# Sums of squares made inside the output products, one phase for two norms, and a new order in the products' opening turns

## Chip, core and metric

The kernel runs on one core of a Trainium2 chip. The time is device microseconds of one launch. A profiled execution gives a second number, its span, from the first to the last instruction of the program. Engines: PE is TensorE, DVE is VectorE, ACT is ScalarE, POOL is GpSimd, SP is SyncE, which issues most loads.

## The reference

Two blocks in a row on 512 tokens of width 1024, all in float32. The first puts 16 meta tokens ahead (528 tokens), runs a pooling mixer and an HGRN2 mixer, each on the RMS norm of the residual stream `h`, and norms the result. The second computes six modulation vectors from `c`, then attention and a product-key expert layer (PEER), each on a modulated norm.

```python
for i in range(DEPTH):                       # first block
    hn = rmsnorm(h, norm_w[i])
    h = h + (pool_mixer if i == 0 else hgrn2_mixer)(hn, ...)   # each ends in (...) @ w_out
x = rmsnorm(h[:, N_META:], final_norm_w)
mod = silu(c) @ w_ada + b_ada                # second block
h1 = rmsnorm(x, norm1_g) * (1.0 + scale1) + shift1
x = x + gate1 * (attention(h1) @ w_o)
h2 = rmsnorm(x, norm2_g) * (1.0 + scale2) + shift2
x = x + gate2 * peer(h2, ...)
```

with `rmsnorm(x, w) = x * rsqrt(mean(x * x) + EPS) * w`, the mean over the 1024 features of a token.

## The kernel before

Activations lie transposed: features on the 128 partitions, `KC` = 8 chunks of them, tokens along the free side. `hT` is `h` (8 x 528), `xT` is `x` (8 x 512). The program is a row of phases. Each has one instruction block per engine and ends in a barrier of all engines, so the next phase begins when the last engine is through. In order: load, scalars, norm0, pool, **pool_out**, **norm1**, hgrn, **hgrn_out**, gains, **final** norm, **mod1**, latent, two phases of attention heads, **attn_out**, **mod2**, peer (1369 of the 3219 us). The bold ones are touched.

`norm_phase` (L249) is one norm. ScalarE squares the even chunks (L274), VectorE squares the odd ones and adds each pair (L300, L302), TensorE multiplies a matrix of ones with the four pair sums (L292), which leaves the sum over features on every partition. Then ScalarE takes the root (L276), VectorE the reciprocal (L304) and scales the 8 chunks (L306). In mod1 and mod2 ScalarE adds a shift to each chunk (L281). In norm1 it makes the high part of each (L285; a float32 is split into two rounded parts), and the low parts are subtractions, chunks 0 to 3 on GpSimd (L318) and 4 to 7 on VectorE (L311).

`product_phase` (L328) multiplies a weight matrix with the mixer's output and adds the product to the residual, in 8 turns m of 128 output features. `kc` is 16 in pool_out and hgrn_out, 8 in attn_out. Per turn: SP loads w(m) (L364) and, where modulation is computed ("ada"), two pieces of `w_ada` (L369), the second only when VectorE has used up the previous turn's; ScalarE makes the high part wh(m) (L408); GpSimd subtracts for the low part wl(m) (L423); TensorE makes three products for each k, wh x rh, wh x rl, wl x rh (L394), once wl(m) is there; VectorE makes ada(m) in 8 chained operations (L453, L455), then adds the product to the residual, in two halves of 264 tokens (L1983, attn_out: L2052 with a gate), and an ada result of 3 columns to `mod` (L442). Two w buffers: w(m+2) is issued when wl(m) is done, but it stands in SP's queue behind both ada pieces of turn m+1. The high parts rh of the right side come from ScalarE before turn 1 (L411), the low parts rl from VectorE, all 16 or 8 of them, before its ada(0) (L434); in turn 0 TensorE waits for rl k by k.

## Time and profile before

| | us |
|---|---|
| median of 3 runs (range) | 3217.63 (3217.52 to 3218.79) |
| the profiled execution: time, span | 3220.95, 3219.2 |
| pool_out, from its first load to the next phase | 285.5 to 409.5 |
| norm1, up to hgrn's first instruction | 409.5 to 433.5 |
| hgrn_out with gains | 1150.5 to 1275.3 |
| final and mod1, up to latent's first matmul | 1275.3 to 1310.7 |
| attn_out | 1775.1 to 1831.2 |
| mod2, up to peer's first matmul | 1831.2 to 1849.6 |
| peer | 1849.6 to 3219 |
| busy: TensorE, VectorE, GpSimd, ScalarE | 79%, 66%, 36%, 31% of the span |

A timeline row gives start and length in us, engine, line, operation, tile written <- tiles read, shape, count; in square brackets the idle time ahead of it and what ended that. Rows of one kind in a row are merged, so a length can cover several instructions with what they waited for. A length holds the time from an instruction's start to its end, also when it stands still between.

### The profile page before, as it was taken

To read this page: it belongs to the slowest core of one execution; us is meant where nothing else is said; L and a number is where in the kernel's file an instruction comes from. 1 tells how busy PE (TensorE), PEld (TensorE's weight loads), DVE (VectorE), ACT (ScalarE), POOL (GpSimd) and SP (SyncE) were. 2 spreads that over 40 slices of the span, in tenths; PEclk is the share of its full clock that TensorE was granted. 3 is DMA by queue.
4 is the path that set the end of the run, shared out by engine and by line. 5 is a ranking of instruction groups with operands and counts; after the bars stand their busy time and mean duration, and the time that the engine had idled before them with its cause. 6 is when DMAs were issued, how large, how long until landed. Compare 5 with 4: busy or idle time off the path is not lost. (4 is left out here: it accounts for less than half of the span.)

```text
span 3219.2 us, 36203 instructions
## 1 busy us (share of the span) xinstructions
PE 2555.9 (79%) x12276; PEld 1759.3 (55%) x12276; DVE 2108.6 (66%) x3964; ACT 997.9 (31%) x2010; POOL 1170.2 (36%) x952
## 2 busy tenths in 40 slices
PE   6998969999999968767799688966766677766676
PEld 5998959889988858324466533322322232222222
DVE  6356646666666675466534327788887788878876
ACT  2222145555555521232223212222222222222221
POOL 2443345555455522011100214444444444444442
PEclk8999988889898979878899899998888888888888
DMA  3233621111111034100110249999999999999998
GB/s 99 87 95 99 190 59 50 43 52 46 52 52 46 27 122 140 39 28 0 40 40 1 79 171 400 415 427 427 410 427 426 423 403 427 427 420 402 427 423 341
DMA packets 269757, 666.41 MB, mean 207 GB/s; under 512 B 13989, under 2 KB 201546, under 8 KB 203834
## 3 DMA queue, kind: packets, MB, share of 16 engines
q0 software_dynamic: 73728, 536.90, 39.9%
q1 hardware_dynamic: 194906, 127.75, 13.2%
q8 instruction: 68, 1.11, 0.1%
q14 instruction: 63, 0.52, 0.0%
q10 hardware_dynamic: 992, 0.13, 0.0%
HBM read 662.64 MB, written 2.10 MB: 206 GB/s over the span
## 5 line engine op out<-in xcount | busy, mean ns | idle before, releaser
L1898 PE MATMUL peer_py<-peer_uv,peer_diag 128*128 128x512 f32 x1536 | 852.0, 703 | 348.4 <-ACT peer_diag L1828 348.2
L1616 POOL DMA_INDIRECT peer_uv<-k_peer_uv,peer_idx x512 | 510.8, 998 | 773.3 <-PE peer_py L1898 710.7
L1898 PEld LDWEIGHTS peer_py<-peer_uv,peer_diag 128*128 128x128 f32 x1536 | 324.4, 223 | 842.2 <-issue 835.1
L1718 DVE SCALAR_TENSOR_TENSOR peer_spare<-peer_uv,peer_hp 128x1024 bf16<-128x1024 f32 x512 | 622.8, 1217 | 226.2 <-DMA peer_uv<-k_peer_uv,peer_idx 225.4
L1820 ACT ACTIVATE peer_ga<-peer_a 128x2 f32<-128x2 f32 x256 | 52.0, 203 | 827.3 <-DVE peer_spare L1718 827.3
L862 PE MATMUL hgrn_pp<-p2n_hh,hgrn_wh 128*128 128x264 f32 x1024 | 227.2, 305 | 27.6 <-POOL hgrn_wl L733 27.6
L733 POOL TENSOR_TENSOR hgrn_wl<-p2n_w,hgrn_wh 128x1024 fp32r<-128x1024 f32 x64 | 153.8, 2403 | 183.7 <-ACT hgrn_wh L770 183.7
L862 PE MATMUL hgrn_pp<-p2n_hl,hgrn_wh 128*128 128x264 f32 x1024 | 218.6, 296 | 0.0
L862 PE MATMUL hgrn_pp<-p2n_hh,hgrn_wl 128*128 128x264 f32 x1024 | 217.2, 295 | 0.0
L862 PEld LDWEIGHTS hgrn_pp<-p2n_hh,hgrn_wh 128*128 128x128 f32 x1024 | 171.7, 204 | 28.8 <-POOL hgrn_wl L733 28.2
L1828 ACT ACTIVATE peer_diag<-keep_ident,peer_wt 128x128 f32<-128x128 f32 x384 | 140.3, 396 | 113.7 <-DVE peer_wt L1725 109.8
L862 PEld LDWEIGHTS hgrn_pp<-p2n_hl,hgrn_wh 128*128 128x128 f32 x1024 | 170.4, 202 | 0.0
L862 PEld LDWEIGHTS hgrn_pp<-p2n_hh,hgrn_wl 128*128 128x128 f32 x1024 | 168.1, 199 | 0.0
L592 POOL TENSOR_TENSOR pool_wl<-p1n_w,pool_wh 128x1024 fp32r<-128x1024 f32 (+1 forms) x48 | 100.6, 2096 | 179.6 <-ACT pool_wh L567 179.6
L1740 DVE SCALAR_TENSOR_TENSOR peer_part<-peer_uv,peer_wt,peer_part 128x1024 f32<-128x1024 f32 x124 | 159.5, 1286 | 4.6 <-DVE peer_wt L1725 0.2
L747 POOL TENSOR_TENSOR hgrn_kq<-hgrn_q,hgrn_e 128x264 f32<-128x264 f32 (+1 forms) x112 | 111.1, 992 | 130.7 <-ACT hgrn_e L780 130.7
L890 PE MATMUL hgrn_pS<-hgrn_kq 128*128 128x64 f32 x896 | 120.7, 291 | 44.2 <-DVE hgrn_prod L1034 43.6
L890 PEld LDWEIGHTS hgrn_pS<-hgrn_kq 128*128 128x128 f32 x896 | 115.3, 207 | 48.1 <-issue 37.8
L1000 DVE TENSOR_TENSOR hgrn_dif<-hgrn_b 128x528 f32<-128x528 f32 (+1 forms) x112 | 112.0, 1030 | 24.7 <-ACT hgrn_e L780 19.8
L1855 PE MATMUL peer_pQ<-p_h,p_w 128*128 128x512 f32 x256 | 115.6, 605 | 13.4 <-PEq L109 10.7
L553 PE MATMUL pool_ps<-pool_xh,pool_wh 128*128 128x264 f32 x512 | 105.4, 287 | 16.6 <-DVE pool_xl L604 14.3
L748 POOL TENSOR_TENSOR hgrn_kq<-hgrn_k,hgrn_e 128x264 f32<-128x264 f32 (+1 forms) x112 | 115.3, 1029 | 0.0
(371 smaller groups left out, 4850.4 us busy)
## 6 DMA issues: line engine op xcount, KB each, us to landing
p2n_w<-in_hgrn_w_in SPq DMA_DIRECT2D x64, 512.0 KB, 3.9
p1n_w<-in_pool_w_in SPq DMA_DIRECT2D x32, 512.0 KB, 3.9
pool_out_aw<-in_w_ada SPq DMA_DIRECT2D x16, 768.0 KB, 4.7
hgrn_out_aw<-in_w_ada SPq DMA_DIRECT2D x16, 768.0 KB, 4.7
pool_out_w<-in_pool_w_out SPq DMA_DIRECT2D x8, 1024.0 KB, 7.0
hgrn_out_w<-in_hgrn_w_out SPq DMA_DIRECT2D x8, 1024.0 KB, 7.3
p_w<-in_w_pq SPq DMA_DIRECT2D x8, 1024.0 KB, 6.3
peer_uv<-k_peer_uv,peer_idx POOLq DMA_INDIRECT x512, 12.1
```

The costliest lines, as they stand in the source:

```text
L733: pool.tensor_tensor(wl[:, part % 2], w[:, part % 2], wh[:, part % 2].bitcast(F32), ALU.subtract)\
L747: pool.tensor_tensor(to[:, :, d:], blocks(q[:, b], d, at)[:, :, d:], e[:, :, d:], ALU.mult)
L748: pool.tensor_tensor(to[:, :, :d], blocks(k[:, b], d, at)[:, :, :d], e[:, :, :d], ALU.mult)\
L862: last = pe.matmul(pp[:, slot, h, 0:HALF], x[:, slot, c, :], y[:, c, h * HALF:(h + 1) * HALF], start=c == 0 and j == 0, stop=c == KC - 1 a ...
L890: last = pe.matmul(pS[:, l % 2, j * (P // 2):(j + 1) * (P // 2)], kq[:, l - 1, t], seconds(kq[:, l - 1, t], LEVELS[l - 1]), start=True, st ...
L1000: dve.tensor_tensor(blocks(dif[:, l % 2], d, at), x, x[:, :, d - 1:d].to_broadcast([P, n_b, 2 * d]), ALU.subtract).then_inc(diff_done, 1)
L1616: pool.indirect_dma_start(out=uv[:, n % DEPTH].rearrange("p w d -> p (w d)"), out_offset=None, in_=io["k_peer_uv"], in_offset=bass.Indirec ...
L1718: dve.scalar_tensor_tensor(out=spare[:, n % 2, :], in0=uv[:, n % DEPTH, 0, :], scalar=1.0, in1=hp[:, t % 2, :], op0=ALU.mult, op1=ALU.mult ...
L1740: dve.scalar_tensor_tensor(out=part[:, :], in0=uv[:, n % DEPTH, 1, :], scalar=wt[:, s, k:k + 1], in1=part[:, :], op0=ALU.mult, op1=ALU.add ...
L1828: act.activation(diag[:, n % DIAGS, :], ident[:, :], ACT.Copy, scale=wt[:, s, k:k + 1])\
L1855: last = pe.matmul(pQ[:, :], w[:, n % 2, c, j * P:(j + 1) * P], h2[:, c, :], start=c == 0, stop=c == KC - 1)
L1898: last = pe.matmul(py[:, h * 512:(h + 1) * 512], diag[:, products(n) % DIAGS, :], uv[:, n % DEPTH, 1, h * 512:(h + 1) * 512], start=n % (P ...
```

## The change

Four things.

- **Sums in the products.** `product_phase` gets `target` and `totals`. Behind each turn's residual addition ScalarE squares the finished chunk (scaled by `final_norm_w` for a second sum in hgrn_out) and GpSimd adds it to a running sum `total` (or `weighted`) of one chunk's size, zeroed at the phase's start. pool_out and attn_out carry one sum, hgrn_out two. norm1 and mod2 take `total` ready: two matmuls with ones, root, and the rest as before. A root of one column (`warm`) stands ahead of ScalarE's wait.
- **One phase for two norms.** `norms_phase` takes the place of final and mod1. The second norm's mean square is `ra*ra*weighted/D`, `ra` being the first's reciprocal root, so both scalings come from `hT`: `hm` with the product of both gains and both roots, `xT` with the first's. A barrier between the two goes.
- **Opening turns.** In turn 0 TensorE makes first all wh x rh as rh arrives, then all wl x rh, then all wh x rl. rl is made by VectorE for k < 10 (5 in attn_out) and by GpSimd for the rest, between wl(0) and wl(1). w(0) of hgrn_out and attn_out is loaded in earlier phases into buffers of its own (in norm1's and norms' load list).
- **Small ones.** In norm1 GpSimd makes 5 low parts and VectorE 3 (4 and 4 before). hgrn uses the kept ones instead of setting its own.

GpSimd, pool_out from its first work (L423 and L526 are wl, L540 rl, L533 the running sum; w0 and w1 the two weight buffers, one tile w before):

```order
L423 TENSOR_TENSOR pool_out_wl<-pool_out_w,pool_out_wh 128x2048 x2
L356 UNCONDITIONAL_BRANCH
L356 ISA
L423 TENSOR_TENSOR pool_out_wl<-pool_out_w,pool_out_wh 128x2048
L422 REGISTER_ALU
L423 TENSOR_TENSOR pool_out_wl<-pool_out_w,pool_out_wh 128x2048
L356 REGISTER_ALU
L356 COMPARE_AND_BRANCH
```

After the change:

```order
L536 MEMSET keep_total 128x528
L526 TENSOR_TENSOR pool_out_wl<-pool_out_w0,pool_out_wh 128x2048
L540 TENSOR_TENSOR pool_out_rl<-p1_u2,pool_out_rh 128x528 x6
L526 TENSOR_TENSOR pool_out_wl<-pool_out_w1,pool_out_wh 128x2048
L543 UNCONDITIONAL_BRANCH
L543 ISA
L526 TENSOR_TENSOR pool_out_wl<-pool_out_w0,pool_out_wh 128x2048
L531 REGISTER_ALU
L533 TENSOR_TENSOR keep_total<-keep_total,pool_out_sq 128x528
L525 REGISTER_ALU
L526 TENSOR_TENSOR pool_out_wl<-pool_out_w1,pool_out_wh 128x2048
```

Six rl now stand between wl(0) and wl(1), and in the loop an addition stands behind each wl.

VectorE, the end of the final norm and the start of mod1, before (L304 the reciprocal, L306 the scalings, L109 and L296 the way to the next phase):

```order
L302 TENSOR_TENSOR final_sq<-final_sq 128x512
L304 RECIPROCAL final_rs<-final_rs 128x512
L306 SCALAR_TENSOR_TENSOR keep_xT<-first_hT,keep_cols,final_rs 128x512 x8
L109 UNCONDITIONAL_BRANCH
L296 UNCONDITIONAL_BRANCH
L300 TENSOR_TENSOR mod_sq<-keep_xT 128x512
L302 TENSOR_TENSOR mod_sq<-mod_sq 128x512
```

VectorE's whole norms phase after (L370 and L379 the reciprocals, L376, L382 and L385 the scalings):

```order
L368 TENSOR_TENSOR norms_both_gains<-keep_cols 128x8
L370 RECIPROCAL norms_ra<-norms_ra 128x512
L373 TENSOR_TENSOR norms_rb<-norms_ra,norms_ps 128x512
L374 TENSOR_TENSOR norms_rb<-norms_rb,norms_ra 128x512
L376 SCALAR_TENSOR_TENSOR keep_xT<-first_hT,keep_cols,norms_ra 128x512 x4
L379 RECIPROCAL norms_rb<-norms_rb 128x512
L380 TENSOR_TENSOR norms_rab<-norms_ra,norms_rb 128x512
L382 SCALAR_TENSOR_TENSOR p_hm<-first_hT,norms_both_gains,norms_rab 128x512 x8
L385 SCALAR_TENSOR_TENSOR keep_xT<-first_hT,keep_cols,norms_ra 128x512 x4
```

The squares and pair sums are gone, two reciprocals and sixteen scalings stay, and four of the scalings moved ahead of the second reciprocal.

```diff
@@ norm_phase(..., total=None)
+            if total is None:
+                for c in range(0, KC, 2):
+                    act.activation(sq[:, c], x[:, c, 0:tokens], ACT.Square).then_inc(squared, 1)
+            else:
+                act.activation(warm[:, :], keep["eps"][:, 0:1], ACT.Sqrt)
             act.wait_ge(summed, 1)
...
+            if total is not None:
+                for h in range(2):
+                    last = pe.matmul(ps[:, h, 0:half], keep["ones"][:, :], total[:, h * half:(h + 1) * half],
+                                     start=True, stop=True)
+            for c in range(1, KC if total is None else 1, 2):
...
-                for c in range(KC // 2, KC):
+                for c in range(5, KC):
@@ norms_phase, new
+            for j, t in enumerate((total, weighted)):
+                pe.matmul(ps[:, j, :], keep["ones"][:, :], t[:, META:T], start=True, stop=True).then_inc(summed, 1)
...
+            act.activation(ra[:, :], ps[:, 0, :], ACT.Sqrt, bias=keep["eps"][:, 0:1], scale=1.0 / D).then_inc(rooted, 1)
+            act.wait_ge(scaled, 1)
+            act.activation(rb[:, :], rb[:, :], ACT.Sqrt, bias=keep["eps"][:, 0:1], scale=1.0 / D).then_inc(rooted, 1)
+            for c in range(KC):
+                act.wait_ge(scaled, c + 2)
+                act.activation(out[:, c, :], out[:, c, :], ACT.Identity, bias=shift(c))
...
+            ch.link(dve.reciprocal(ra[:, :], ra[:, :]))
...
+            ch.link(dve.tensor_tensor(rb[:, :], ra[:, :], ps[:, 1, :], ALU.mult))
+            dve.tensor_tensor(rb[:, :], rb[:, :], ra[:, :], ALU.mult).then_inc(scaled, 1)
+            for c in range(KC // 2):
+                dve.scalar_tensor_tensor(out=x[:, c, :], in0=h[:, c, :], scalar=weight[:, c:c + 1], in1=ra[:, :],
+                                         op0=ALU.mult, op1=ALU.mult)
+            dve.wait_ge(rooted, 2)
+            ch.link(dve.reciprocal(rb[:, :], rb[:, :]))
+            ch.link(dve.tensor_tensor(rab[:, :], ra[:, :], rb[:, :], ALU.mult))
...
@@ product_phase(..., ada=None, early=None, target=None, totals=())
+    by_dve = kc * 5 // 8
...
-                sp.wait_ge(wl_done, m + 1)
-                sp.dma_start(w[:, b], view[:, :, ds(m * P, P)]).then_inc(w_in[b], 16)
+                if not (first and early):
+                    sp.wait_ge(wl_done, m + 1)
+                    sp.dma_start(w[b], view[:, :, ds(m * P, P)]).then_inc(w_in[b], 16)
...
+                if first:
+
+                    pe.wait_ge(wh_done, 1)
+                    for j, (x, y) in enumerate(((wh, rh), (wl, rh), (wh, rl))):
+                        if j == 1:
+                            pe.wait_ge(wl_done, m + 3)
+                        for k in range(kc):
+                            if j == 0:
+                                pe.wait_ge(rh_done, k + 1)
+                            elif j == 2 and k < by_dve:
+                                pe.wait_ge(rl_done, k + 1)
+                            elif j == 2:
+                                pe.wait_ge(rl_done2, k - by_dve + 1)
+                            last = products(b, k, j, x, y)
...
+            def squares(m, b):
+
+                for j, (gain, total) in enumerate(totals):
+                    if j == 0:
+                        act.wait_ge(taken, (m + 3) * nsp)
+                        act.wait_ge(sq_added, (m + 1) * nt)
+                    act.activation(sq[:, j], target(m), ACT.Square, scale=gain(m) if gain else 1.0)\
+                       .then_inc(sq_done, 1)
...
+            def add(m, b):
+
+                for j, (gain, total) in enumerate(totals):
+                    pool.wait_ge(sq_done, m * nt + (j + 1))
+                    pool.wait_ge(sq_added, m * nt + (j + 1))
+                    pool.tensor_tensor(total[:, :], total[:, :], sq[:, j], ALU.add).then_inc(sq_added, 1)
+
+            for gain, total in totals:
+                pool.memset(total[:, :], 0.0).then_inc(sq_added, 1)
+            low(0, 0)
+            for k in range(by_dve, kc):
+                pool.wait_ge(rh_done, k + 1)
+                pool.tensor_tensor(rl[:, k], rhs[:, k, 0:tokens], rh[:, k].bitcast(F32), ALU.subtract)\
+                    .then_inc(rl_done2, 1)
+            low(1, 1)
+            with pool.Fori(0, turns // 2 - 1) as i:
+                for b in range(2):
+                    low(i * 2 + (2 + b), b)
+                    add(i * 2 + b, b)
+            add(turns - 2, 0)
+            add(turns - 1, 1)
```

In the code before and after, `step(m, ...)` of the loops runs m = 2 to 7 in three passes of two.

## Rows read from the trace of the kernel before

**Rows 1.** The page's DMA issues: line, count, KB each, us to landing.

```profile
pool_out_w<-in_pool_w_out SPq DMA_DIRECT2D x8, 1024.0 KB, 7.0
```

**Rows 2.** Timeline from pool_out's end into norm1: start, length, instruction [idle before]; a POOL group.

```profile
407.30 0.77 DVE L1983 TENSOR_TENSOR first_hT<-pool_out_ps,first_hT 128x264 f32 x2 [6.54 <-PE pool_out_ps L394]
...
408.43 0.16 DVE L442 TENSOR_TENSOR keep_mod<-pool_out_pa,keep_mod 128x3 f32<-128x3 f32 x1 [0.28 <-PE pool_out_pa L382]
...
409.59 2.24 ACT L274 ACTIVATE norm_sq<-first_hT 128x528 f32<-128x528 f32 x4 [19.57 <-PEq L95]
...
411.85 1.28 ACT L276 ACT_TABLE_LOAD   x1
...
416.77 0.70 ACT L276 ACTIVATE norm_rs<-norm_ps,keep_eps 128x528 f32<-128x528 f32 x1 [3.64 <-PE norm_ps L292]
...
422.58 6.93 POOL L318 TENSOR_TENSOR p2n_hl<-p2h_hn,p2n_hh 128x528 fp32r<-128x528 f32 x4 [27.88 <-ACT p2n_hh L285]
...
L1411 POOL TENSOR_TENSOR fox_sq<-fox_raw 128x512 f32<-128x512 f32 x8 | 8.3, 1038 | 158.6 <-ACT fox_raw L1436 158.6
```

**Rows 3.** Timeline of the final norm, mod1 and the next phase; a DMA's landing.

```profile
1275.36 2.19 ACT L274 ACTIVATE final_sq<-first_hT 128x512 f32<-128x512 f32 x4 [24.26 <-PEq L95]
...
1283.64 3.35 DVE L304 RECIPROCAL final_rs<-final_rs 128x512 f32<-128x512 f32 x1 [2.49 <-ACT final_rs L276]
...
1287.03 5.39 DVE L306 SCALAR_TENSOR_TENSOR keep_xT<-first_hT,keep_cols,final_rs 128x512 f32<-128x512 f32 x8
...
1310.68 14.68 PE L1139 MATMUL latent_pr<-p_hm,p3l_w 128*128 128x512 f32 x28 [10.65 <-PEq L109]
...
p3l_w<-in_w_in SPq DMA_DIRECT2D x1, 2688.0 KB, 9.6
```

**Rows 4.** Timeline of mod2, the norm behind attn_out.

```profile
1831.26 2.19 ACT L274 ACTIVATE mod_sq<-keep_xT 128x512 f32<-128x512 f32 x4 [12.02 <-PEq L95]
...
1836.37 0.69 DVE L302 TENSOR_TENSOR mod_sq<-mod_sq 128x512 f32<-128x512 f32 x1
...
1838.99 0.69 ACT L276 ACTIVATE mod_rs<-mod_ps,keep_eps 128x512 f32<-128x512 f32 x1 [4.24 <-PE mod_ps L292]
```

**Rows 5.** Timeline of pool_out's opening turns, VectorE, GpSimd, SP's queue and TensorE.

```profile
292.69 4.52 POOL L423 TENSOR_TENSOR pool_out_wl<-pool_out_w,pool_out_wh 128x2048 fp32r<-128x2048 f32 x1 [12.03 <-ACT pool_out_wh L408]
...
293.18 13.87 DVE L434 TENSOR_TENSOR pool_out_rl<-p_u,pool_out_rh 128x528 fp32r<-128x528 f32 x16 [7.96 <-ACT pool_out_rh L411]
...
303.02 8.50 POOL L423 TENSOR_TENSOR pool_out_wl<-pool_out_w,pool_out_wh 128x2048 fp32r<-128x2048 f32 x1 [5.82 <-ACT pool_out_wh L408]
...
311.77 4.66 DVE L455 SCALAR_TENSOR_TENSOR pool_out_acc<-pool_out_aw,keep_silu_c,pool_out_acc 128x384 f32<-128x384 f32 x7
...
317.27 0.39 SPq L364 DMA_DIRECT2D pool_out_w<-in_pool_w_out  x1
...
326.57 13.04 DVE L455 SCALAR_TENSOR_TENSOR pool_out_acc<-pool_out_aw,keep_silu_c,pool_out_acc 128x384 f32<-128x384 f32 x7
...
331.03 0.80 PE L394 MATMUL pool_out_ps<-pool_out_rh,pool_out_wh 128*128 128x264 f32 x2 [6.90 <-POOL pool_out_wl L423]
```

**Rows 6.** Timeline: the openings of hgrn_out (upper two) and attn_out.

```profile
1150.58 0.37 SPq L364 DMA_DIRECT2D hgrn_out_w<-in_hgrn_w_out  x1
...
1155.92 1.91 ACT L408 ACTIVATE hgrn_out_wh<-hgrn_out_w 128x2048 fp32r<-128x2048 f32 x1 [10.65 <-DMA hgrn_out_w<-in_hgrn_w_out]
...
1779.32 1.06 ACT L408 ACTIVATE attn_out_wh<-attn_out_w 128x1024 fp32r<-128x1024 f32 x1 [4.42 <-DMA attn_out_w<-in_w_o]
...
1790.98 0.75 DVE L2052 SCALAR_TENSOR_TENSOR keep_xT<-attn_out_ps,keep_mod,keep_xT 128x512 f32<-128x512 f32 x1 [1.23 <-PE attn_out_ps L394]
```

**Rows 7.** Timeline of VectorE in a later turn of hgrn_out.

```profile
1247.21 0.77 DVE L1983 TENSOR_TENSOR first_hT<-hgrn_out_ps,first_hT 128x264 f32 x2 [6.54 <-PE hgrn_out_ps L394]
...
1248.66 8.89 DVE L455 SCALAR_TENSOR_TENSOR hgrn_out_acc<-hgrn_out_aw,keep_silu_c,hgrn_out_acc 128x384 f32<-128x384 f32 x7
...
1259.70 0.77 DVE L1983 TENSOR_TENSOR first_hT<-hgrn_out_ps,first_hT 128x264 f32 x2 [2.15 <-PE hgrn_out_ps L394]
```

More of the change, by code:

```diff
@@ L257, in norm_phase @@
     with Phase(nc, name) as ph:
-        sq = ph.sb("sq", [P, KC, tokens])
-        rs = ph.sb("rs", [P, tokens])
+        sq = ph.sb("sq", [P, KC if total is None else 1, tokens])
+        rs, warm = ph.sb("rs", [P, tokens]), ph.sb("warm", [P, 1])
         ps = ph.ps("ps", [P, 2, 512])
@@ L298, in _ @@
             ch = Chain(dve, own)
-            for c in range(1, KC, 2):
+            for c in range(1, KC if total is None else 1, 2):
                 ch.link(dve.tensor_tensor(sq[:, c], x[:, c, 0:tokens], x[:, c, 0:tokens], ALU.mult))
@@ L315, in _ @@
             if halves:
-                for c in range(KC // 2):
+                for c in range(5):
                     pool.wait_ge(high_done, c + 1)
@@ L384, in partitions, with products @@
                 last.then_inc(a_summed, 1)
+            def products(b, k, j, x, y):
+                for s, (at, n) in enumerate(spans):
+                    last = pe.matmul(ps[:, b, s, 0:n], x[:, b, k, :], y[:, k, at:at + n],
+                                     start=k == 0 and j == 0, stop=k == kc - 1 and j == 2)
+                return last
             def step(m, b, i, first):
-                pe.wait_ge(wl_done, m + 3)
                 pe.wait_ge(taken, (m + 1) * nsp)
-                for k in range(kc):
-                    if first:
-                        pe.wait_ge(rl_done, k + 1)
-                    for j, (x, y) in enumerate(((wh, rh), (wh, rl), (wl, rh))):
-                        for s, (at, n) in enumerate(spans):
-                            last = pe.matmul(ps[:, b, s, 0:n], x[:, b, k, :], y[:, k, at:at + n],
-                                             start=k == 0 and j == 0, stop=k == kc - 1 and j == 2)
+                if first:
[11 more added lines that the diff above has]
+                            last = products(b, k, j, x, y)
+                else:
+                    pe.wait_ge(wl_done, m + 3)
+                    for k in range(kc):
+                        for j, (x, y) in enumerate(((wh, rh), (wh, rl), (wl, rh))):
+                            last = products(b, k, j, x, y)
                 last.then_inc(summed, 1)
@@ L415, in _ @@
                     high(i * 2 + (2 + b), b, i + 1)
+                    squares(i * 2 + b, b)
+            squares(turns - 2, 0)
+            squares(turns - 1, 1)
         @blk.gpsimd
@@ L431, in _ @@
                 dve.sem_inc(aw_used, 2)
-            for k in range(kc):
+            for k in range(by_dve):
                 dve.wait_ge(rh_done, k + 1)
@@ L1983, in residual, with rows @@
                 return dve.tensor_tensor(h, sums, h, ALU.add)
+            total, weighted = keep["total"], ph0.sb("weighted", [P, T])
+            def rows(m):
+                return hT[:, ds(m, 1), :].rearrange("p a t -> p (a t)")
             with Phase(nc, "p1") as ph1:
@@ L1997, in program @@
                     pool_phase(nc, io, keep, hn, u2, w, w_in)
-                product_phase(nc, "pool_out", io["pool_w_out"][0], EC, u2, spans, residual, keep, (io["w_ada_2"], 0))
+                product_phase(nc, "pool_out", io["pool_w_out"][0], EC, u2, spans, residual, keep, (io["w_ada_2"], 0),
+                              target=rows, totals=[(None, total)])
             show("h1", hT[:, :, :])
@@ L2017, in hgrn_ahead, with final_weight @@
                             sp.dma_start(masks[:, :, :], io["k_masks"]).then_inc(masks_in, 16)
[L2018 removed]
+                            sp.dma_start(wo[:, :, :], io["hgrn_w_out"][0].rearrange("(k p) n -> p k n", p=P)[:, :, 0:P])\
+                              .then_inc(wo_in, 16)
+                        norm_phase(nc, "norm1", hT, hn, col("norm_w", KC), T, halves=(hh, hl), ahead=hgrn_ahead,
+                                   total=total)
                     hgrn_phase(nc, io, keep, hh, hl, og, w, w_in, masks, masks_in)
[L2020 removed]
+                def final_weight(m):
+                    return cols[:, ds(m + COL["final_norm_w"], 1)]
+                product_phase(nc, "hgrn_out", io["hgrn_w_out"][0], EC, og, spans, residual, keep, (io["w_ada_2"], 1),
+                              early=(wo[:, :, :], wo_in), target=rows, totals=[(None, total), (final_weight, weighted)])
             gains_phase(nc, keep)
```

121 lines of the change are left out of this document (78 added, 43 removed).

## The prediction, made before the changed kernel ran

> **What bounds the kernel now.** The page's busy shares come first: no engine fills the span, so chains of waits set the end, stage by stage. The change touches only what stands in three output products and in four norms, and there a barrier closes each phase: whatever ends last in a phase moves everything behind it, one for one. So I read the timeline of those phases alone and sum what each one's end moves. "Turn" is one of a product's eight steps m; wh, wl, rh, rl are the high and low parts of weights and right side; "ada" is the 8-operation sum that VectorE makes in each turn of the two products that carry it.
>
> A norm is a chain that nothing overlaps: in norm1 the squares start at 409.59 and the square root waits until 416.77 [rows 2]; mod2 has the same gap, 1831.26 to 1838.99 [rows 4]. The final norm and mod1 together take from 1275.36 to 1310.68, 35.3 us [rows 3].
>
> In the opening of pool_out the thing to see is the pairing of VectorE and GpSimd [rows 5]. GpSimd makes wl(0) from 292.69 to 297.21; VectorE's 16 rl, "running" since 293.18, end at 307.05, which is 9.84 us or 0.615 each counted from 297.21: the first stood still until GpSimd was done. Then the reverse: wl(1) is issued at 303.02 and takes 8.50 instead of 4.52 and so ends 4.47 after VectorE's last rl. The two never progress together. After that ada(0) ends at 316.43 (311.77 and 4.66), the load of w(2) is issued behind it in SP's queue at 317.27, and TensorE starts product 2 at 331.03 after idling 6.90. **The end of ada(0) sets product 2**, 14.6 us later.
>
> **The sums leave the norms.** norm1: instead of 4+4 squares, adds and 16 matmul passes, two matmuls on a ready sum. Before, the root began 7.2 after the phase's start. After, I take 1.9: in mod2 that lies between VectorE's last add, 1837.06, and the root, 1838.99, with two matmuls between them [rows 4]. Less than about 1.5 it can't be, since the warm root brings its table load of 1.28 in front [rows 2]. Gain 5.3. One low part goes from VectorE to GpSimd: a pair in that stretch takes 1.73 (6.93 for 4 [rows 2]), of which 0.62 is VectorE's, so GpSimd's part costs 1.1 and VectorE's 0.65 goes: +0.3, with high parts from ScalarE as the pace. Net **-5.0**. mod2: 7.73 becomes 1.9, **-5.8**.
>
> norms phase, from its start: root A at 1.9, 0.7 long [rows 4], reciprocal 3.35 [rows 3], two products 1.4 (0.69 each [rows 4]), four scalings 2.7 (5.39 for 8 [rows 3]; root B is hidden behind them), reciprocal 3.35, one product 0.7, eight scalings 5.39, four 2.7, hand-overs and barrier 0.7: 22.9. ScalarE's shifts run beside the last twelve. Against 35.3, **-12.4**. The phase's weights took 9.6 us to land [rows 3], and 22.9 are there even with the 0.5 MB that now stand between them (a fifth of 2.7 MB, some 2 us, which is what it costs if uncovered): nothing.
>
> **The sums arrive in the products.** Tail: after the last residual, ScalarE squares (0.56, a quarter of 2.24 [rows 2]) and GpSimd adds (1.04 for 512 elements [rows 2]; 1.1 with 528). So far the end was VectorE's own rest of 0.5 behind that residual, 408.07 to 408.59 [rows 2]. pool_out: 0.1+0.6+0.1+1.1-0.5 = +1.4. hgrn_out has two sums, the second add behind the first: +2.6. attn_out has no rest: +1.8.
>
> In the turns the adds stand on GpSimd behind wl(m+2), where VectorE wants to do ada. A turn is 12.5 us (1247.21 to 1259.70 [rows 7]). VectorE's ada is 5.05 long undisturbed (0.4+4.66 [rows 5]); with wl in its middle the seven take 8.89 [rows 7]. The chain from a residual to a product two turns on is: 1.0, ada 5.05, issue 0.9 [rows 5], landing 7.0 [rows 1], wh 2.0 [rows 6], wl 4.6 [rows 5]: 20.6, and it may last 24.9. A blocked ada adds 4.2: 24.8, so in such turns the slack is nil; an unblocked one leaves 4. In every second or third turn the add lands within a blocked ada. pool_out: 1.1 each; following the turns once through, only the load of w(6) comes late, by 1.6. hgrn_out: 2.2 each, which delays w(4) by 2.4 and w(6) by 3.6 in the worst order; I take 4.5. Bounds: 0 (adds fall where VectorE waits for TensorE, 6.5 us in some turns [rows 7]) to 3 and 7. So **+1.6 and +4.5**. In attn_out a turn of 5.5 (seven between 1790.98 [rows 6] and 2 us before 1831.26 [rows 4]) holds 2.4 (half a wl) + 1.1 of GpSimd and no ada: nothing.
>
> **The opening turns.** TensorE's new order lets the high products run while terms arrive, but product 0 was not the bound: ada(0) was, and after it w(2). What changes there is that six rl go from VectorE at 0.615 to GpSimd at 1.1. Since the two take turns, the queue up to ada(0)'s end is a plain sum whichever goes first: 10x0.615 + 6x1.1 + wl(1) 4.5 + ada 5.0 = 22.2 from wl(0)'s end, against 19.2 measured. pool_out: **+2.9**. hgrn_out has w(0) loaded ahead: its wh(0) waited from 1150.58 to 1155.92, so 5.3 goes and 2.9 comes [rows 6]: **-2.4**. attn_out: wh(0), idle for 4.42 and begun at 1779.32, begins 4.1 earlier and wl(0) ends at 1778.7; behind it 5x0.6 + 3x1.1 + 2.4 give wl(1) at 1787.4, where product 1 had been able to start at 1790.98 [rows 6]: **-3.5**. If a stream of ada holds GpSimd off, as the rl held wl(1) in [rows 5], w(2) comes early but wl(1) late, and product 2 moves by only +1.8 and -4.5.
>
> On this the Trainium skill has a rule, page "SBUF — State Buffer", section "Who interferes with whom": a VectorE instruction with two SBUF inputs and a GpSimd instruction that reads SBUF exclude each other for a whole instruction, so splitting a stream between them cannot overlap it. It speaks against this edit, and [rows 5] agree in that VectorE's rl fit into 9.84 us only if it stood still for GpSimd's 4.52; the page's "starts first" doesn't cover the 8.50. By rule and rows the opening is +2.9; with side-by-side work it would be the second rival below.
>
> **The sum**, against the profiled span of 3219.2 (a run's time is about 1.7 above its span, the median 3217.63 lies 1.6 below the span; a difference carries over unchanged): pool_out 2.9+1.6+1.4 = +5.9; norm1 -5.0; hgrn_out -2.4+4.5+2.6 = +4.7; norms -12.4; attn_out -3.5+1.8 = -1.7; mod2 -5.8. Total -14.3: 3217.6-14.3 = **3203.3 us**. The long peer stage shifts as a whole.
>
> **Rivals.** (1) The adds are hidden: if they fall in VectorE's wait for TensorE, 6.1 goes and 3197 is left. For it: unblocked turns show 6.5 us of such waiting; against: blocked adas with nil slack [rows 7]. (2) VectorE and GpSimd do overlap on these shapes: then rl would be ready by 304 and ada(0) by 305, product 1 starts when wl(1) is done at 308.4 and product 2 at 320.8, 10.2 earlier than before instead of 2.9 later; the same in hgrn_out, 2 in attn_out, no stalls: 14.3+13.1+13.1+6.1+2 = 48.6, or 3169. Nothing in the trace speaks for it; the 13.87 and the 8.50 speak against. (3) Slower: a second wl falls into the ada as well, as it does once in pool_out, where the seven operations take 13.04 [rows 5]. Then the chain is 20.6 + 2x4.2, and with both turns' adds, 2.2 or 4.4, it is 31.2 and 33.4 against 24.9. It would bind in every third turn, twice in each product: 2x6.3 + 2x8.5 = 29.6 in place of the 6.1, and the total is +9.2: 3226.8. The sign turns once the two products stall by 20.4 in all. Against it: it happens once, in the turn whose load came late behind the opening, and an ada delayed in one turn finds GpSimd free in the next. (4) The change doesn't take the root's wait away, because total is late at the barrier: that is the tail, already counted; nothing else feeds the two matmuls.
>
> **How the numbers follow.** Forecast 0.69, rival 1 0.21, rival 2 0.05, rival 3 0.05. The range runs from rival 1 with the better order in the openings (3194) to the forecast with stalls of 3 and 7, the ones' matmuls half a microsecond later in each norm and a slower split (3210). 0.2% is 6.4 us, about what measurement of this kernel can tell from no change: faster below 3211.2. Of the forecast's share I leave 0.08 above that. Faster 0.87, same 0.09, slower 0.04.
>
> **What the profile after would show.** Root of norm1 and mod2 1.9 after their phase's start; norms phase near 22.9; last add of total about 2 us behind the last residual; product 2 of pool_out 36.7 us behind the end of wl(0) (33.8 before), with VectorE or GpSimd instructions standing still for 4.5 us beside a wl; TensorE idle before one or two later products. I am wrong if product 2 of pool_out starts earlier than now, if adas in the turns are longer by more than 2.3, or if the norms' weights land after its scalings.

## The result, and the profile after

The change made the kernel slower. The median of seven runs is 3231.7 us (3225.4 to 3234.2), that of the kernel before beside it 3217.6 (3216.9 to 3220.2): a ratio of 1.0038, with a 95% interval of 1.0026 to 1.0049. The prediction was 3203.3 us, with a range of 3194 to 3210, and 0.87 for faster. The profiled execution has a span of 3232.4 us, against 3219.2.

A table of stages, read as the time from a stage's first instruction to that of the next, shows where it went (us; the column "aligned" belongs to an experiment below, the other two are the profiled executions of before and after):

| stage | before | after | difference | predicted | aligned |
|---|---|---|---|---|---|
| up to pool_out | 285.5 | 286.2 | +0.7 | 0 | 284.0 |
| pool_out | 124.1 | 132.4 | +8.4 | +5.9 | 129.9 |
| norm1 and the hgrn stage | 741.0 | 736.0 | -5.0 | -5.0 | 734.8 |
| hgrn_out | 124.8 | 134.0 | +9.2 | +4.7 | 133.3 |
| final and mod1, or the norms phase | 35.3 | 22.8 | -12.5 | -12.4 | 22.8 |
| latent and the heads | 464.5 | 468.6 | +4.1 | 0 | 468.9 |
| attn_out and mod2 | 74.4 | 67.6 | -6.8 | -7.5 | 67.6 |
| peer | 1369.6 | 1384.7 | +15.1 | 0 | 1367.4 |

Each column is one execution. In all the kernels of this document the stretch up to pool_out takes 283.5 to 286.2 us and the hgrn stage, without norm1, 713.3 to 717.8, with nearly the same instructions in them. So 3 or 4 us in one of these stages show nothing by themselves. The peer stage with its tiles in their old place takes 1366.1 to 1369.6.

The norms did what was forecast. In mod2 of the kernel after, with start, length, line and tiles as in [rows 4]:

```profile
1835.09 1.01 SPq L2210 DMA_DIRECT2D p_w<-in_w_pq  x2
1835.10 1.28 ACT L277 ACT_TABLE_LOAD   x1 [2.57 <-PEq L95]
1835.13 2.04 PE L294 MATMUL mod_ps<-keep_total,keep_ones 128*128 128x256 f32 x4 [4.27 <-PEq L95]
1837.22 0.69 ACT L279 ACTIVATE mod_rs<-mod_ps,keep_eps 128x512 f32<-128x512 f32 x1 [0.62 <-PE mod_ps L294]
```

The root starts 2.1 us behind the phase's start, where it was 7.7 in [rows 4]. norm1 alone, up to hgrn's first instruction, takes 19.3 us for 23.9. In the norms phase, which answers to [rows 3], the phase's first and last pieces are

```profile
1288.69 0.38 SPq L2178 DMA_DIRECT2D p3l_w<-in_w_in  x1
1290.82 0.69 ACT L358 ACTIVATE norms_ra<-norms_ps,keep_eps 128x512 f32<-128x512 f32 x1 [1.90 <-PE norms_ps L352]
1308.51 2.73 DVE L385 SCALAR_TENSOR_TENSOR keep_xT<-first_hT,keep_cols,norms_ra 128x512 f32<-128x512 f32 x4
1311.50 0.34 SPq L1250 DMA_DIRECT2D latent_pos_i<-in_positions  x1
```

which is 22.8 us. Up to the first instruction of peer, the kernel after was even 1.9 us ahead (1847.7 against 1849.6). **It is the last stage, which the change doesn't touch, that made it slower.** Its instructions are the same; what differs is how fast the rows arrive that GpSimd gathers (128 rows of 8 KB each time, into the buffer peer_uv). Of both kernels, the stretch from 2100 to 3100 us (its length, GpSimd's busy time, TensorE's granted clock, the DMA engines' busy share, GB/s), first before, then after:

```profile
2100.00:3100.00 1000.00, 422.38 (x424) 0.86 1.00 421
```

```profile
2100.00:3100.00 1000.00, 408.50 (x416) 0.87 1.00 415
```

The DMA engines are busy all the time in both, and move 1.4% less after the change. In the view of the tile peer_uv for that stretch (behind the x the count of GpSimd's gathers, then least, median and longest ns of issuing one), again before and after:

```profile
L1616 POOL DMA_INDIRECT peer_uv<-k_peer_uv,peer_idx x399: 932/936/1946, 2099.2 to 3098.1; - x200
```

```profile
L1739 POOL DMA_INDIRECT peer_uv<-k_peer_uv,peer_idx x392: 932/936/1997, 2103.3 to 3096.0; - x196
```

GpSimd issues one in the same 936 ns, but there are 392 in the time of 399: it waits longer until rows have been used, since those come later. The engines that read the buffer are no slower: in the same views one matmul on it takes 592 ns (median) and one of VectorE's products 1220 ns in both kernels.

The opening of pool_out, beside [rows 5]: VectorE's ten low parts, GpSimd's six, wl(1), the end of ada(0), the load of w(2), the landing and the product.

```profile
293.79 4.56 POOL L526 TENSOR_TENSOR pool_out_wl<-pool_out_w,pool_out_wh 128x2048 fp32r<-128x2048 f32 x1 [6.97 <-ACT pool_out_wh L498]
294.28 21.27 DVE L558 TENSOR_TENSOR pool_out_rl<-p_u,pool_out_rh 128x528 fp32r<-128x528 f32 x10 [8.36 <-ACT pool_out_rh L511]
299.66 10.40 POOL L540 TENSOR_TENSOR pool_out_rl<-p_u,pool_out_rh 128x528 fp32r<-128x528 f32 x6 [1.30 <-ACT pool_out_rh L511]
310.03 4.96 POOL L526 TENSOR_TENSOR pool_out_wl<-pool_out_w,pool_out_wh 128x2048 fp32r<-128x2048 f32 x1
315.92 4.65 DVE L579 SCALAR_TENSOR_TENSOR pool_out_acc<-pool_out_aw,keep_silu_c,pool_out_acc 128x384 f32<-128x384 f32 x7
321.41 0.39 SPq L437 DMA_DIRECT2D pool_out_w<-in_pool_w_out  x1
330.54 1.91 ACT L498 ACTIVATE pool_out_wh<-pool_out_w 128x2048 fp32r<-128x2048 f32 x1 [26.48 <-DMA pool_out_w<-in_pool_w_out]
337.24 0.81 PE L461 MATMUL pool_out_ps<-pool_out_rh,pool_out_wh 128*128 128x264 f32 x2 [5.68 <-POOL pool_out_wl L526]
```

wl(0) ends at 298.35, ada(0) at 320.57: 22.2 us, as the sum of the queue had it. Ten low parts of VectorE now take 21.27 us, more than sixteen took before (13.87), since the last of them waits for GpSimd's row. But from ada(0)'s end to product 2 there are 16.7 us, not 14.6: w(2) needed 9.1 us from issue to wh, and 7.0 before.

A blocked turn of hgrn_out, beside [rows 7]. While VectorE makes its seven operations, GpSimd has one wl (as in [rows 7]) and four adds, and the seven take 12.64 us instead of 8.89. The third and fourth add begin at 1237.04 and 1238.64; the wl at 1223.24 is over before the seven begin.

```profile
1223.24 4.56 POOL L526 TENSOR_TENSOR hgrn_out_wl<-p_wo,hgrn_out_wh 128x2048 fp32r<-128x2048 f32 x1 [12.43 <-ACT hgrn_out_wh L498]
1227.75 1.44 POOL L533 TENSOR_TENSOR keep_total<-keep_total,hgrn_out_sq 128x528 f32<-128x528 f32 x1
1228.05 12.64 DVE L579 SCALAR_TENSOR_TENSOR hgrn_out_acc<-hgrn_out_aw,keep_silu_c,hgrn_out_acc 128x384 f32<-128x384 f32 x7
1229.15 1.64 POOL L533 TENSOR_TENSOR first_weighted<-first_weighted,hgrn_out_sq 128x528 f32<-128x528 f32 x1
1232.41 4.67 POOL L526 TENSOR_TENSOR hgrn_out_wl<-hgrn_out_w,hgrn_out_wh 128x2048 fp32r<-128x2048 f32 x1 [1.62 <-ACT hgrn_out_wh L498]
1241.85 0.37 SPq L437 DMA_DIRECT2D p_wo<-in_hgrn_w_out  x1
1255.97 0.81 PE L461 MATMUL hgrn_out_ps<-hgrn_out_rh,hgrn_out_wh 128*128 128x264 f32 x2 [3.18 <-POOL hgrn_out_wl L526]
```

SP issues w(6) (written to the tile p_wo) only at 1241.85, behind a piece of `w_ada` that waits for the end of that ada (1240.69), although wl(4), which freed the weight buffer, ended at 1227.80. TensorE stands for 3.18 us.

### The profile page after: what moved, and what is told of

Same layout as the page of the kernel before. It is cut to its first block and busy times, and to the rows that moved or that the text cites. A ratio compares the mean times of both kernels' runs of the same rounds, so it can differ in the third digit from the quotient of the medians.

```text
span 3232.4 us, 36212 instructions
## 1 busy us (share of the span) xinstructions
PE 2542.1 (79%) x12224; PEld 1749.8 (54%) x12224; DVE 2111.0 (65%) x3919; ACT 1008.8 (31%) x2029; POOL 1228.4 (38%) x1004
## 5 line engine op out<-in xcount | busy, mean ns | idle before, releaser
L2021 PE MATMUL peer_py<-peer_uv,peer_diag 128*128 128x512 f32 x1536 | 838.6, 693 | 378.5 <-ACT peer_diag L1951 359.1
L1739 POOL DMA_INDIRECT peer_uv<-k_peer_uv,peer_idx x512 | 501.3, 979 | 799.1 <-PE peer_py L2021 744.2
L1978 PE MATMUL peer_pQ<-p_h,p_w 128*128 128x512 f32 x256 | 115.1, 603 | 13.3 <-PEq L109 10.6
```

What stands on the lines that cost most here:

```text
L1739: pool.indirect_dma_start(out=uv[:, n % DEPTH].rearrange("p w d -> p (w d)"), out_offset=None, in_=io["k_peer_uv"], in_offset=bass.Indirec ...
L1978: last = pe.matmul(pQ[:, :], w[:, n % 2, c, j * P:(j + 1) * P], h2[:, c, :], start=c == 0, stop=c == KC - 1)
L2021: last = pe.matmul(py[:, h * 512:(h + 1) * 512], diag[:, products(n) % DIAGS, :], uv[:, n % DEPTH, 1, h * 512:(h + 1) * 512], start=n % (P ...
```

## Experiments

Fourteen kernels ran, in four groups that each shared a chip with runs of the kernel before (medians 3219.6, 3220.0, 3219.6, 3219.3). Kernels named b_ are edits of the kernel before, those named a_ of the kernel after.

### The place of the tiles

The new tile total takes 2112 bytes of every partition, 64 more than a multiple of 512, and stands ahead of all that is allocated later. peer_uv began at byte 67584 of a partition before, a multiple of 512, and begins at 69696 after.

**b_shift2112**: only a hole of that size in the kernel before.

```diff
-            ..., "xT": ph.sb("xT", [P, KC, SEQ]),
+            ..., "xT": ph.sb("xT", [P, KC, SEQ]), "pad": ph.sb("pad", [P, T]),
```

> The kernel before, with one unused tile of 528 floats per partition behind xT, which moves every later tile up by 2112 bytes, as the new tile total does; no instruction differs. Theory P (the place of the tiles): the gathers of the peer stage write rows that begin 64 bytes behind a multiple of 512 and run at some 421 GB/s in place of 427 as in the kernel after, so the peer stage takes 13 to 15 us more, the latent and head stages up to 4 more, and the time is 3232 to 3237. Rival T (the peer stage is longer in the kernel after because of when it starts, or through a state left behind by the new phases): no instruction and no start differs here, so the time is that of before, 3216 to 3220.

3241.4 us, a ratio of 1.0069 (1.0052 to 1.0086), 4 us above the range of theory P. Not an instruction differs, and the peer stage takes 1386.1 us, 16.5 more than before; pool_out takes 1.4 more and hgrn_out 2.1, the latent and head stages the same 464.6. Rival T has fallen, and so has theory P's part on the heads.

**b_uv64** moves one tile; **b_uv128** and **b_uv256** differ from it in the two sizes (32 and 96, 64 and 64 floats).

```diff
+        ph.sb("pad0", [P, 16])
         uv = ph.sb("uv", [P, DEPTH, 2, D])
+        ph.sb("pad1", [P, 112])
```

> The kernel before, with 64 unused bytes ahead of the gather buffer peer_uv and 448 behind it, so that peer_uv alone begins 64 bytes behind a multiple of 512 and all tiles behind it keep their place to 512 bytes. Theory P: all of the 13 to 15 us of the peer stage, and nothing ahead of it: 3230 to 3233. If the place of the tiles matters through what the engines read (skT, qT, the small tiles) and not through the gather's rows: 3217 to 3219. Rival T: 3217 to 3219.

> As b_uv64, with peer_uv 256 bytes behind a multiple of 512. If rows must begin on a multiple of 512 bytes: as b_uv64, 3233 to 3240. If a multiple of 256, or of less above 64, is enough: 3216 to 3221.

> As b_uv64 and b_uv256, with peer_uv 128 bytes behind a multiple of 512. If rows must begin on a multiple of 128 bytes: as the kernel before, 3216 to 3221. If they must begin on a multiple of 256: as b_uv64, 3233 to 3240.

b_uv64: 3237.1 us (ratio 1.0054, 1.0037 to 1.0070), again 4 us above its range. b_uv256: 3220.3 (0.9999, 0.9990 to 1.0009). b_uv128: 3235.9 (1.0052, 1.0035 to 1.0068). The same stretch of the three, for 64, 128 and 256 bytes behind a multiple of 512:

```profile
2100.00:3100.00 1000.00, 410.28 (x418) 0.86 1.00 415
```

```profile
2100.00:3100.00 1000.00, 408.39 (x417) 0.87 1.00 415
```

```profile
2100.00:3100.00 1000.00, 422.12 (x424) 0.87 1.00 420
```

So the gather buffer's place alone costs what the peer stage lost, at 64 and at 128 bytes alike (1384.3 and 1384.6 us), and nothing at 256 (1369.6). Of the two readings set down for 128 bytes, the one by which 128 is enough is out. The Trainium skill, page "DMA: Bandwidth & Descriptors", section "How a descriptor splits into AXI transactions", says that the first piece of a transfer must begin at a multiple of 256 bytes, so that one which starts between two multiples also pays for the bytes ahead of its start. It says so of reading; here it is the written side that moved. The boundary agrees with the four places measured (0, 64, 128 and 256 bytes behind a multiple of 512), and the price was 1.4% of the rate. That the page's rule is the reason on the written side is not shown.

**b_shift512**, the same hole with 512 bytes:

> The kernel before, with one unused tile of 512 bytes per partition behind xT: all later tiles move, but keep their place to a multiple of 512 bytes, and lose it to 2048. Theory P with a grain of 512 bytes or finer: as before, 3216 to 3220. Theory P with a grain of 2048 bytes: the peer stage is longer by some 14 us, 3230 to 3237. Rival T: 3216 to 3220.

3220.4 us, ratio 1.0002 (0.9992 to 1.0011). It isn't the moving that costs.

**a_p4pad** and **a_aligned** undo the displacement in the kernel after. a_p4pad has one line:

```diff
         with Phase(nc, "p4") as ph4:
+            ph4.sb("pad", [P, 112])
             h2 = ph4.sb("h2", [P, KC, SEQ])
```

a_aligned has this and a hole of 112 floats ahead of load_xrows and of 96 ahead of u2, of hgrn_out's tiles and of hm.

> The kernel after with 448 unused bytes ahead of the peer stage's tiles and no other padding, so that peer_uv, h2 and w begin on a multiple of 512 again. If the peer stage's loss is the place of its own buffers: its stretch from the first peer instruction to the end falls from 1384.6 us to 1367 to 1370, all other stages are those of the kernel after, and the time is 3213 to 3218, between the kernel after (3232) and a_aligned (3208). If the stages ahead of it matter to it: above 3225.

> The kernel after, with unused padding of 384 or 448 bytes ahead of the load phase's tiles, the pool mixer's, hgrn_out's, the attention stage's and the peer stage's, so that their weight and gather buffers have the place to 512 bytes that they had before; no instruction differs. Theory P: the peer stage gives back 13 to 15 us, the latent and head stages up to 4, and the slower landings in the two big openings a microsecond or two: 3211 to 3217. Rival T: as the kernel after, 3226 to 3234.

a_p4pad: 3212.7 us, ratio 0.9977 (0.9966 to 0.9988), peer stage 1368.2. a_aligned: 3208.2, ratio 0.9963 (0.9951 to 0.9976), peer stage 1367.4. Each against the kernel before of its own group, the kernel after is 14.1 us slower, a_p4pad 6.6 faster and a_aligned 11.4 faster. One unused tile turns the slower kernel into a faster one: of 25.5 us, 20.7 come back with it. In the profiled executions, which differ by 19.0, 16.5 lie in the peer stage; the rest lies ahead of it, where the two kernels are alike, and is no more than executions differ. From a_p4pad to a_aligned, pool_out gives the largest part. pool_out went from 132.4 in the kernel after to 129.9 in a_aligned; the median landing of its weights on the page is 8.0 in the kernel after and 7.2 in a_aligned. The head stage didn't give its 4 us back, so that part of theory P was wrong.

### The turns of the two big products

All from here on a_aligned, 3208.2 us.

**a_noadd** leaves GpSimd's adds out:

```diff
-                    pool.tensor_tensor(total[:, :], total[:, :], sq[:, j], ALU.add).then_inc(sq_added, 1)
+                    pool.sem_inc(sq_added, 1)
```

> a_aligned with GpSimd's adds to the running sums left out (the squares stay; the sums stay zero, so the norms scale by another factor). Theory G (GpSimd's adds, 1.4 to 1.65 us each, make its weight halves late and stretch VectorE's chain beside them): both stalls of hgrn_out (1.0 and 2.9 us) and the slower clock behind them (3 us) go, and the tails of the three phases shorten by 1.3 to 4 us each: 3194 to 3199. Rival Q (the stalls are the weight load's, which SyncE issues behind the waits of the ada loads): only the tails go, 3202 to 3205.

3198.7 us, ratio 0.9933 (0.9917 to 0.9950), as theory G had it. hgrn_out went from 133.3 to 126.6, pool_out from 129.9 to 128.1, and the longest stall in their turns is 0.6 us; the wait for product 2 stays (4.5 and 5.5 us).

**a_sp** lets SP issue a weight load ahead of the ada loads of the turn in front:

```diff
-            def step(m, b, i, first):
-                ...
-            walk(sp, step)
+            if not early:
+                load_w(0, 0)
+            load_w(1, 1)
+            load_aw(0)
+            with sp.Fori(0, turns // 2 - 1) as i:
+                for b in range(2):
+                    load_w(i * 2 + (2 + b), b)
+                    load_aw(i * 2 + (1 + b))
+            load_aw(turns - 1)
```

> a_aligned, with SyncE issuing the weight load of turn m+1 ahead of the ada loads of turn m (it waits for its buffer alone, not behind VectorE's chain). Rival Q: w(2) of the two big phases is issued some 4 us earlier and w(4) and w(6) some 5, the stalls of hgrn_out go with the slower clock behind them (7 us), and the second products start 2 to 4 us earlier: 3196 to 3203. Theory G: GpSimd's row of halves and adds is as long as before, the stalls stay, and only the openings gain: 3204 to 3207.

3184.4 us, ratio 0.9893 (0.9877 to 0.9910): more than either theory said. hgrn_out takes 119.3 us, 14.0 less than in a_aligned, pool_out 122.9, 7.0 less. TensorE idles neither ahead of product 2 nor in the turns, though GpSimd still has its adds. wl(4) of hgrn_out, then VectorE, GpSimd and SP a turn later:

```profile
1195.32 4.62 POOL L539 TENSOR_TENSOR hgrn_out_wl<-p_wo,hgrn_out_wh 128x2048 fp32r<-128x2048 f32 x1 [4.78 <-ACT hgrn_out_wh L511]
1207.17 0.77 DVE L2119 TENSOR_TENSOR first_hT<-hgrn_out_ps,first_hT 128x264 f32 x2 [0.42 <-DVE hgrn_out_acc L592]
1207.72 4.62 POOL L539 TENSOR_TENSOR hgrn_out_wl<-hgrn_out_w,hgrn_out_wh 128x2048 fp32r<-128x2048 f32 x1 [4.77 <-ACT hgrn_out_wh L511]
1207.90 0.37 SPq L439 DMA_DIRECT2D p_wo<-in_hgrn_w_out  x1
1212.29 1.44 POOL L546 TENSOR_TENSOR keep_total<-keep_total,hgrn_out_sq 128x528 f32<-128x528 f32 x1
1213.69 1.64 POOL L546 TENSOR_TENSOR first_weighted<-first_weighted,hgrn_out_sq 128x528 f32<-128x528 f32 x1
```

w(2) is issued as soon as wl(0) frees its buffer (1148.80, behind 1148.62). The later loads are not: w(6) goes at 1207.90, 8.0 us after wl(4) freed the buffer, since it still stands behind ada pieces, only those of one turn earlier. The expectation had them wait for their buffer alone. That one turn is enough: product 6 begins at 1230.90, and wl(6) is ready at 1224.73. Taking either away, the adds or SP's old order, takes nearly all the stall in the turns away: each lay on the path only through the other. A stall can also cost twice. In a_aligned product 6 of hgrn_out starts at 1249.0 after 2.9 us of idleness; a stretch of TensorE ahead of it, one behind it and the next (busy time, granted clock, DMA share, GB/s; a transfer counts whole where it starts, so a share can pass 1):

```profile
1236.00:1246.00 10.00, 10.00 (x85) 1.00 1.07 348
1249.00:1255.00 6.00, 6.00 (x27) 0.50 0.00 0
1255.00:1263.00 8.00, 8.00 (x67) 0.99 0.30 99
```

Six microseconds at half clock are three more lost. The two stalls of hgrn_out in a_aligned (1.0 and 2.9) and this are the 6.9 us by which its turns are longer than before. The stall of 1.0 cost hardly more than itself: from product 3 to product 4 there are 13.6 us, where an undisturbed one takes 12.4.

**b_sp**, the same order in the kernel before:

> The kernel before with SyncE's order of a_sp alone. Theory (the weight load of turn 2 stands behind the ada loads in the kernel before too, and TensorE idles 6.9 and 6.7 us for it [rows 5]): both idle times go, no other stage changes, 3204 to 3208. Rival (the order only hurts where the sums' adds and the stretched chain of VectorE stand in the way, in the kernel after): 3216 to 3220.

3200.4 us, ratio 0.9938 (0.9922 to 0.9955), more than expected: pool_out 115.0 (124.1 before) and hgrn_out 116.1 (124.8). Product 2 had started late in both, and the clock was low behind its wait. Of before (first two) and of b_sp, TensorE in the turn behind product 2's start and in the turns after:

```profile
331.00:345.30 14.30, 14.27 (x100) 0.83 0.47 148
345.30:407.00 61.70, 61.70 (x510) 1.00 0.53 162
```

```profile
322.00:334.40 12.40, 12.40 (x105) 1.00 1.08 350
334.40:396.00 61.60, 61.60 (x510) 1.00 0.59 180
```

Product 2 takes 14.6 us in the kernel before (331.03 to 345.62) and 12.4 in b_sp. So the wait for w(2) in pool_out cost 9.1 us, 6.9 of idle time and 2.2 of slow clock behind it. It has nothing to do with the change, and mending it brings more (19.2 us) than the change was forecast to (14.3).

**a_rl_vector** gives the split low parts back to VectorE:

```diff
-    by_dve = kc * 5 // 8
+    by_dve = kc
```

> The kernel after with its tiles aligned (a_aligned, 3208 us), and all low halves rl of the three openings on VectorE as before (16 or 8 of them); the early first weights and the sums stay. Theory S (the split itself costs: 10 subtractions of VectorE beside 6 of GpSimd took 21.3 us, where VectorE alone had 16 in 13.9 us): the second product of pool_out starts some 3.7 us earlier, and that of hgrn_out 3 to 5, so 3200 to 3203. Rival W (the weight path sets the start of product 2 anyway, since wl(1) on GpSimd runs beside the subtractions and takes 8.5 us as before): within 2 us of a_aligned, 3206 to 3210.

3200.1 us, ratio 0.9936 (0.9920 to 0.9953). pool_out takes 126.6 us, 3.3 less, hgrn_out 129.4, 3.9 less, and attn_out with mod2 1.3 less: theory S. VectorE has its sixteen in 13.93 us again, and wl(1) its 8.48:

```profile
293.16 13.93 DVE L561 TENSOR_TENSOR pool_out_rl<-p_u,pool_out_rh 128x528 fp32r<-128x528 f32 x16 [7.97 <-ACT pool_out_rh L514]
303.02 8.48 POOL L529 TENSOR_TENSOR pool_out_wl<-pool_out_w,pool_out_wh 128x2048 fp32r<-128x2048 f32 x1 [5.78 <-ACT pool_out_wh L501]
```

### The head stage and the clock

In a_rl_vector the latent and head stages take 464.7 us and in a_aligned 468.9, though the norms phase ahead of them and they themselves have the same instructions. The whole difference lies in the first of the two head phases, 214.3 us against 209.9; the latent stage takes 68.4 and 68.1, the second head phase 186.2 and 186.7. TensorE in that first head phase, a_aligned and then a_rl_vector, has as many matmuls and a lower clock where it is longer:

```profile
1373.20:1587.50 214.30, 165.17 (x576) 0.79 0.04 11
```

```profile
1365.50:1575.40 209.90, 161.87 (x576) 0.81 0.04 11
```

TensorE in the latent stage's first 4 us and in four stretches of the heads, counted from the stage's start alike, a_aligned and then a_rl_vector:

```profile
1304.80:1309.00 4.20, 4.18 (x5) 0.50 0.31 88
1394.80:1424.80 30.00, 17.38 (x35) 0.66 0.06 19
1424.80:1454.80 30.00, 25.30 (x89) 0.80 0.06 19
1454.80:1484.80 30.00, 26.36 (x77) 0.74 0.00 1
1484.80:1514.80 30.00, 21.03 (x83) 0.77 0.00 0
```

```profile
1297.50:1301.70 4.20, 4.20 (x5) 0.50 0.32 88
1387.40:1417.40 30.00, 18.52 (x41) 0.72 0.06 18
1417.40:1447.40 30.00, 21.74 (x86) 0.85 0.06 19
1447.40:1477.40 30.00, 27.53 (x105) 0.92 0.00 1
1477.40:1507.40 30.00, 21.05 (x69) 0.66 0.00 1
```

The granted clock falls in both, at other places. The profiled executions lie in two groups: 464 to 466 us (before, all b_ kernels, a_rl_vector, a_sp, a_best) and 467.5 to 469 (after, a_aligned, a_p4pad, a_noadd).

**a_fill** gives TensorE work ahead of them:

```diff
+            for _ in range(40):
+                pe.matmul(ps[:, 2, :], keep["ones"][:, :], total[:, META:T], start=True, stop=True)
```

> a_aligned with 40 idle matmuls (ones by total, into a spare PSUM bank, read by nobody) behind the two sums in the norms phase, so that TensorE is busy until about the phase's end instead of idle for 19 us. Theory C (the 4.2 us that the latent and head stages are longer in the kernel after are TensorE's clock, which falls at other places of the same instructions because TensorE did other work ahead of them): the latent stage's first 4 us, at a granted clock of 0.50 in both kernels, run at 1.0 and save 2 us, and the head stage changes its length by a microsecond or more either way, for a stretch from the latent phase to attn_out other than 281.2 us. Rival L (the 4.2 us come from late landings or another engine): that stretch is 283.2 less 2.0 = 281.2 us within 0.5.

3222.4 us: the 40 took longer than I had reckoned and the norms phase grew by 15.7 us. What was asked is answered all the same. The latent and head stages take 462.9 us, 6.0 less than in a_aligned; 2.4 of these lie in the latent stage, with its first stretch at full clock, and 3.8 in the first head phase. (The 283.2 and 281.2 us of the expectation are not the stretch up to attn_out, which is 468.9; with 2.0 less, rival L's would be 466.9.) Rival L is out, and theory C holds as far as this: the length of the first head phase moves by some 4 us with what TensorE did ahead of the stage, and the granted clock in it goes with that. What decides where it falls is open; it isn't the stage's start alone (1311.43 in b_shift512 with 464.9, 1311.50 in the kernel after with 468.6).

### Put together

**a_best** is a_sp with a_rl_vector's edit, **a_best_fill** that with 20 idle matmuls instead of 40.

> a_sp (3184 us) with all low halves rl on VectorE (the edit of a_rl_vector). If the two edits take different waits away (a_sp the wait for w(2), w(4) and w(6), this one the wait of product 0 for the last low halves, 6.2 us in each of the two big openings where a_rl_vector has 2.2): 4 us less in each and 1 in attn_out, 3174 to 3178. Rival (in a_rl_vector the split cost through the weight path, which a_sp has already freed): 3181 to 3185.

> The kernel of a_best with 20 idle matmuls behind the sums of the norms phase (the 40 of a_fill took 36 us and made that phase 15.7 us longer; 20 should end at about its end). Theory C: the first 4.3 us of the latent stage run at a granted clock of 1.0 instead of 0.50 and save 2.2 us, the head stage changes its length by some microseconds either way, and no other stage does; 2 to 6 us less than a_best. Rival: the matmuls delay the phase's end or change nothing, from 1 us less to 2 us more than a_best.

a_best: 3182.6 us, ratio 0.9884 (0.9867 to 0.9900), 1 to 2 us below a_sp where 6 to 10 were expected, and so within the rival's range. By stages it is the theory that holds: pool_out gave 4.7 and hgrn_out 3.2. But norm1 and hgrn took 3.2 more and the heads 1.3 more in the profiled execution. In the hgrn stage that is again TensorE: for the same 4880 matmuls it is busy for 645.4 us at a granted clock of 0.90 in a_sp, and for 648.4 at 0.89 in a_best. a_best_fill: 3177.9 us (3175.1 to 3179.4), ratio 0.9866 (0.9850 to 0.9883), the fastest kernel here: latent and heads 462.4 against 465.7, and in the latent stage's first stretch

```profile
1282.40:1286.60 4.20, 4.18 (x10) 1.00 0.31 88
```

ten matmuls at full clock in the time of five. The intervals of the two ratios overlap, the runs themselves don't (a_best 3180.5 to 3183.2). The profiled executions differ by 1.3 us only, because hgrn_out, with the same instructions, took 119.3 us here and 116.2 in a_best: VectorE's last addition began 4.3 us behind TensorE's last product there, and 1.3 in a_best. Why is open.

## Why the prediction was wrong

**The step that failed** is the last sentence under the sum, "The long peer stage shifts as a whole": +15.1 us where it had 0. I costed instructions and none was added there. What the runs showed in its place is a gather that fills its buffer at 415 instead of 421 GB/s because the buffer begins 64 bytes behind a multiple of 256. The new tile was followed as a value that engines read and write, not as bytes that displace all tiles behind it. b_shift2112, with no instruction changed, shows it. With the displacement undone (a_aligned) the kernel is 11.4 us faster than before, where 14.3 was forecast; its 3208.2 us lie in the stated range, in part by luck: pool_out and hgrn_out take 5.8 and 8.5 more than before for 5.9 and 4.7, the heads 4.4 more for 0, and stages that the change leaves alone happen to be shorter.

Point by point, by the prediction's own steps:

- **Norms.** -5.0, -12.4 and -5.8 were forecast. norm1 gave -4.6, the norms phase -12.5, mod2 -5.7 (18.3 to 12.6) and attn_out -1.1 for -1.7. The roots start 2.1 to 2.2 behind the phase instead of 1.9. Right.
- **Tails.** From the last residual to the next phase pool_out takes 3.9 us and hgrn_out 5.7, against 2.3 and 3.3: +1.6 and +2.5, for +1.4 and +2.6. Right. In attn_out it was +2.0 for +1.8.
- **Openings.** The queue up to ada(0) was right to the tenth, 22.2 us (3.0 more than the 19.2 before, not 2.9), and a_rl_vector shows its price. What was not foreseen is the slower landing of w(2): the opening of pool_out cost 5.5 instead of 2.9 (product 2 38.9 us behind the end of wl(0), where 36.7 was given), of which a_aligned gives 2.0 back. In hgrn_out a_aligned gains 1.0 for 2.4 forecast: its w(2) took 8.6 us to wh where 7.0 was put in (7.5 before). attn_out's opening gave 3.1 for 3.5.
- **Turns.** pool_out lost 0.7 ahead of product 6, for 1.6, and 0.5 more in product 2 itself, at the lower clock. hgrn_out stood still for 4.7 us (3.9 in a_aligned), near the 4.5 put in, but the clock behind the second stall added 3: in a_aligned the term measured 6.9, its upper bound. The mechanism was right, the price of a stall of some 3 us on TensorE was not: as much again came on top. Of product 2 the same holds in part: in the kernel before [rows 5] an idle time of 6.90 was a loss of 9.1. One of my own signs of being wrong came true here, adas longer by more than 2.3: 12.64 for 8.89, with four adds beside it.
- **Latent and heads.** +4.1 for 0, all of it in the first head phase, with the clock low at other places.
- **Rivals.** (2) is refuted: the two engines took turns. (3) came nearest in time, 3226.8, but not as it was meant. An ada made longer by one wl and four adds does occur (12.64 us for the seven), and two wl fall into that of turn 2 as before (17.3 us in hgrn_out, 13.5 before). Yet TensorE stalls for 4.7 us in the turns of hgrn_out and 0.5 in pool_out, and not 29.6. None of the rivals was a change of place, so 0.04 for slower was far too little.

These misses and the forecast add up: -14.3 + 15.1 (peer) + 4.5 (hgrn_out) + 4.1 (heads) + 2.5 (pool_out) + 0.7 (attn_out, mod2) + 0.7 (ahead of pool_out) = +13.3, and the spans differ by 13.2.

With neither in the way, the change is worth about what it was meant to be: a_sp against b_sp, both with tiles in place and SP's order mended, is 35.6 us below its runs of before and the other 19.2: 16.4 us, uncertain by some 7 by the two intervals. Not term by term: 3.6 us of it lie in the hgrn stage, which the change hardly touches.

## What to carry to other kernels

When a change adds or resizes a tile, list where the later tiles begin and keep the destinations of heavy DMA traffic on the multiples that they had (here 256 bytes was enough); a hole of a few hundred bytes is cheap, and an unused tile alone in the old kernel tests it. Look in each issuing queue for a load that stands behind a wait which isn't its own: here moving it brought more than the change. And price a stall of TensorE of some microseconds with the slow clock behind it, not by the idle time alone.
